# Stick-breaking's last gate tile computed among the first scores, and the second local attention's scores two steps at a time with its output projection spread

## The reference, cut to what matters

```python
# stick-breaking attention, per block of 128 queries
logits = jnp.einsum("bhtd,bhsd->bhts", q[:, :, s0:end], kb) * (Dh ** -0.5)
log_keep = jnp.where(mask, jax.nn.log_sigmoid(-logits), 0.0)
after = jnp.sum(log_keep, axis=-1, keepdims=True) - jnp.cumsum(log_keep, axis=-1)
wts = jnp.where(mask, jnp.exp(jax.nn.log_sigmoid(logits) + after), 0.0)
outs.append(jnp.einsum("bhts,bhsd->bhtd", wts, vb))
...
o = o * jax.nn.silu(z)                       # z: the gate, half of a projection of h
return o.astype(h.dtype) @ w_out

# second block
scores = jnp.einsum('nbqhd,nbkhd->nbhqk', qb, kb)      # + bias, softmax, lse
...
y_a = o * jax.nn.silu(g_a)
mixed = jnp.concatenate([y_f, y_a], axis=-1) @ w_out   # y_f: the Fourier half
h = h + mixed
```

## Time and profile before

| | us |
|---|---|
| median of 3 runs | 1233.19 |
| lowest and highest | 1231.24, 1233.85 |
| the profiled execution | 1230.61 |
| its span from first to last instruction | 1228.7 |
| TensorE busy in the span | 1176.3 (96%) |
| ScalarE busy | 538.8 (44%) |
| VectorE busy | 487.4 (40%) |
| GpSimd busy | 370.7 (30%) |

### The profile page before, as it was taken

One profiled execution on the slowest core, in us unless ns is written; L12 is line 12 of the kernel. 1 busy time (PEld: TensorE's weight loads), 2 busy tenths in 40 slices (PEclk: granted clock), 3 DMA queues, 4 the chain that ended last, 5 costly groups with the idle time before them and its releaser, 6 DMA issues.

```text
span 1228.7 us, 21193 instructions
## 1 busy us (share of the span) xinstructions
PE 1176.3 (96%) x8874; PEld 914.7 (74%) x8874; DVE 487.4 (40%) x919; ACT 538.8 (44%) x924; POOL 370.7 (30%) x148
## 2 busy tenths in 40 slices
PE   5999999999989999999999999999999999999998
PEld 3788886677668888777765666888887777777767
DVE  4575544544324472341314553640202332231462
ACT  4232237633336343543547774333125433754430
POOL 0143343132265314344331001332144122333250
PEclk8999999999999999999999999999999999999999
DMA  9723331356650232322422100323132321324201
GB/s 318 231 69 102 102 101 37 103 188 223 208 180 2 69 103 70 102 81 91 129 69 73 26 14 1 124 89 103 34 106 84 111 78 35 103 70 155 87 1 69
DMA packets 105761, 121.14 MB, mean 99 GB/s; under 512 B 5145, under 2 KB 91705, under 8 KB 105673
## 3 DMA queue, kind: packets, MB, share of 16 engines
q1 hardware_dynamic: 101424, 116.14, 29.9%
q10 hardware_dynamic: 4248, 3.73, 1.1%
HBM read 111.47 MB, written 2.10 MB: 92 GB/s over the span
## 4 chain that ended last, share of the span: by engine, by line
PE 84%; ACT 6%; DVE 4%; issue 3%; DMA 1%; ACTq 0%; SPq 0%; POOL 0%; DVEq 0%
PE ps L2039 42%; PE ps L2846 4%; PE ps L2644 3%; PE ps L2635 2%; PE ps L2180 2%; PE ps L2085 2%; PE ps L2426 2%; PE ps L2669 2%; PE ps L2648 1%; PE ps L2778 1%; PE ps L2123 1%; PE ps L2203 1%; PE ps L2256 1%; PE ps L2731 1%; PE ps L2453 1%
## 5 line engine op out<-in xcount | busy, mean ns | idle before, releaser
L604 POOL TENSOR_TENSOR wlo<-raw,whi 128x2048 fp32r<-128x2048 f32 x53 | 245.1, 4624 | 586.1 <-ACT whi L768 571.5
L768 ACT ACTIVATE whi<-raw 128x2048 fp32r<-128x2048 f32 x52 | 99.3, 1911 | 203.2 <-PE ps L2039 164.2
L610 POOL TENSOR_TENSOR wlo<-raw,whi 128x2048 fp32r<-128x2048 f32 x10 | 46.4, 4641 | 111.0 <-ACT whi L857 62.7
L1277 ACT ACTIVATE p<-sc,nmx 128x256 f32<-128x256 f32 x64 | 32.0, 501 | 49.6 <-PE ps L2765 29.5
L857 ACT ACTIVATE whi<-raw 128x2048 fp32r<-128x2048 f32 x11 | 21.1, 1918 | 62.7 <-PE ps L2039 62.7
L2039 PE MATMUL ps<-hC_hi,whi 128*128 128x512 f32 x184 | 47.1, 398 | 0.8 <-POOL wlo L604 0.8
L1861 DVE CUSTOM_DVE_ANT_0 sc<-ps,biast 128x256 f32<-128x256 f32 (+1 forms) x64 | 23.1, 394 | 62.2 <-PE ps L2756 33.3
L2039 PE MATMUL ps<-hC_lo,whi 128*128 128x512 f32 x184 | 45.5, 390 | 0.0
L2039 PE MATMUL ps<-hC_hi,wlo 128*128 128x512 f32 x184 | 45.4, 389 | 0.0
L2039 PEld LDWEIGHTS ps<-hC_hi,whi 128*128 128x128 f32 x184 | 33.8, 188 | 14.9 <-issue 6.4
L2039 PEld LDWEIGHTS ps<-hC_lo,whi 128*128 128x128 f32 x184 | 34.5, 188 | 7.4
(11 more groups left out here) (514 smaller groups left out, 2822.5 us busy)
## 6 DMA issues: line engine op xcount, KB each, us to landing
raw<-in_w_in_dram SPq DMA_DIRECT2D x24, 1024.0 KB, 5.2
raw<-in_w_in_a_dram SPq DMA_DIRECT2D x16, 1024.0 KB, 5.8
raw<-in_w_ada_dram SPq DMA_DIRECT2D x8, 1024.0 KB, 5.5
late_w<-in_w_ada_dram SPq DMA_DIRECT2D x8, 1024.0 KB, 5.5
raw<-in_w_kv_dram SPq DMA_DIRECT2D x8, 1024.0 KB, 5.1
raw<-in_w_in_b_dram SPq DMA_DIRECT2D x8, 1024.0 KB, 5.3
ada_a<-in_w_ada_dram SPq DMA_DIRECT2D x4, 1024.0 KB, 10.0
ada_b<-in_w_ada_dram SPq DMA_DIRECT2D x4, 1024.0 KB, 13.2
```

The costliest lines, as they stand in the source:

```text
L604: pool.tensor_tensor(wlo[:, s, :], raw[:, s, :], whi[:, s, :].bitcast(F32), ALU.subtract).then_inc(lo_ready, 1)
L610: pool.tensor_tensor(wlo[:, s, :], raw[:, s, :], whi[:, s, :].bitcast(F32), ALU.subtract).then_inc(lo_ready, 1)
L768: A(whi[:, s, :], raw[:, s, :], ACT.Copy).then_inc(hi_ready, 1)
L1277: A(p2[:, n % 2, 256 * e:256 * e + 256], sc2[:, n % 2, 256 * e:256 * e + 256], ACT.Exp, scale=-1.0, bias=nmx[:, grp, t, 2 * hp + e:2 * hp ...
```

## The change

1. The last gate tile goes to PSUM bank 7 in three parts of 8 matmuls: ahead of `qk(0)`, between `qk(0)` and `qk(1)`, and behind `qk(1)`. `qk(1)` no longer waits for its copy; DVE copies it after head 0's totals, and `weighted` of pair 1 waits for that copy.
2. ACT's split of the second unit of `D_OUTB` moves from behind head 1's absolute value to behind the exponentials of head 1, in the third turn of the loop.
3. DVE takes the absolute values of heads 0 and 1 ahead of head 0's other work, and the totals lose their two copies: PE now adds two pieces of 128 columns from `att` itself.
4. `weighted` is split as blocks 0 and 3, then 1 and 2.
5. The second window attention takes its scores two steps at a time. The residual of tiles 0 to 2 starts those tiles in its first three pairs, the Fourier half goes in pieces of 6 matmuls, and two thirds of the first `early_rows` fill its last turn. Its shares are begun behind the last copy, and the split of `D_OUT2 + 1` moves one step on.

Two steps' scores stand together, the 12 products are cut in two, and the residual is gone from the middle. The diff, cut to its core:

```diff
 # ScalarE
                 A(later_att(n), later_logits(n), ACT.Abs).then_inc(head_logged, 1)
-                if n == 1:
-                    next_hi(D_ZB + 1, 1)
...
                 if n:
                     head_weights(n - 1)
+                if n == 2:
+                    next_hi(D_ZB + 1, 1)
...
-            window_exps(1, qB, {7: (D_OUT2, 1), 12: (D_OUT2 + 1, 0)}, fourier_hi, stat_exps)
+            window_exps(1, qB, {7: (D_OUT2, 1), 13: (D_OUT2 + 1, 0)}, fourier_hi, stat_exps)
 # VectorE
-                copy(after1[:, 0:128], k2[:, 0:128])
-                TT(after1[:, 128:256], k2[:, 128:256], k3, ALU.add).then_inc(after_step, 1)
-                copy(after0[:, 0:128], k1[:, 0:128])
+                TT(after1[:, 0:128], k2[:, 128:256], k3, ALU.add).then_inc(after_step, 1)
+                TT(after0[:, 0:128], k1[:, 128:256], k2[:, 0:128], ALU.add)
                 dve.wait_ge(after_step, n + 1)
-                TT(after0[:, 128:384], k1[:, 128:384], after1[:, :], ALU.add).then_inc(after_done, 1)
+                TT(after0[:, 128:256], k1[:, 256:384], after1[:, 0:128], ALU.add).then_inc(after_done, 1)
+                if n == 0:
+                    dve.wait_ge(dense_full, 4 * (D_ZB + 2))
+                    dve.wait_ge(gate_done, 7)
+                    copy(zsT[:, KD - 1, :], ps[:, 7, :]).then_inc(gate_done, 1)
...
-                if not grp:
-                    transposed(14)
+                transposed(14)
+                transposed(15)
                 if last:
                     last()
-                transposed(15)
 # TensorE, stick-breaking
-            dense_block(D_ZB + 1, hB)
+            dense_unit(D_ZB + 1, 0, hB)
...
+            products_ch(D_ZB + 1, 1, 0, hB).then_inc(dense_full, 1)
...
+            last_gate(range(8))
...
-                if n < 2:
-                    pe.wait_ge(gate_done, 7 + n)
+                if n == 0:
+                    pe.wait_ge(gate_done, 7)
...
-                later(0, after0[:, :]).then_inc(sfx_first, 1)
-                later(1, after1[:, :])
+                later(0, 128, att(n, off[1], off[1] + 128), 128)
+                later(0, 256, after0[:, :], 256).then_inc(sfx_first, 1)
+                later(1, 128, att(n, off[2], off[2] + 128), 128)
+                later(1, 256, after1[:, :], 128)
...
             qk(0)
+            last_gate(range(8, 16))
             qk(1)
+            last_gate(range(16, 24))
...
-                    weighted((n - 3) // 2, range(1) if n % 2 else range(1, NT))
+                    weighted((n - 3) // 2, (0, 3) if n % 2 else (1, 2))
 # TensorE, the window attention
-                for n in range(18):
-                    if n < 16:
-                        scores(n)
-                        beside(n, 0)
-                    if 1 <= n <= 16:
-                        transposes(n - 1)
-                    if n < 16:
-                        beside(n, 1)
...
+                for m in range(9):
+                    if m < 8:
+                        pair_scores(m)
+                    beside(m, 0)
+                    if m:
+                        transposes(2 * m - 2)
+                    beside(m, 1)
+                    if m:
+                        transposes(2 * m - 1)
+                    beside(m, 2)
...
+                    if m:
+                        weighted_sums(2 * m - 2)
+                        weighted_sums(2 * m - 1)
...
+            def out_rows(m, place):
+
+                if (m, place) in ((0, 0), (1, 1), (2, 1)):
+                    bank_free(D_OUT2, m)
+                    residual(0, m, True)
+                elif 3 <= m <= 6 and place:
...
+                    fourier_rows(m - 3, place - 1)
+                elif (m, place) == (7, 1):
+                    residual(0, 3)
+                elif m == 8 and place:
...
+                    early_rows(0, range(4 * place - 4, 4 * place))
```

More of the change, by code:

```diff
@@ L1777, in yb_low, with magnitudes @@
                 TT(yB_lo[:, kt, :], ybt[:, kt % 2, :], yB_hi[:, kt, :].bitcast(F32), ALU.subtract).then_inc(yblo_done, 1)
-            dve.wait_ge(dense_full, 4 * (D_ZB + 2))
-            dve.wait_ge(gate_done, 7)
-            copy(zsT[:, KD - 1, :], dense[3]).then_inc(gate_done, 1)
-            for n in range(HB):
+            def magnitudes(n):
                 dve.wait_ge(qk_full, n + 1)
@@ L1787, in _ @@
                                   ALU.bitwise_and).then_inc(abs_first, 1)
+            magnitudes(0)
+            for n in range(HB):
+                if n == 0:
+                    magnitudes(1)
+                elif n >= 2:
+                    magnitudes(n)
                 if n >= 5 and n % 2:
@@ L2613, in _, with last_gate @@
             dense_unit(D_ZB, 1, hB, later_sums(SQ_QB + 4, G_QB + 4))
-            dense_block(D_ZB + 1, hB)
+            dense_unit(D_ZB + 1, 0, hB)
+            pe.wait_ge(lo_ready, 2 * (D_ZB + 1) + 2)
+            bank_free(D_ZB + 1, 2)
+            products_ch(D_ZB + 1, 1, 0, hB).then_inc(dense_full, 1)
+            def last_gate(qs):
+                hi, lo = unit(whi, 1, "ch"), unit(wlo, 1, "ch")
+                for q in qs:
+                    which, k = divmod(q, KD)
+                    w, x = ((hi, hB_hi), (lo, hB_hi), (hi, hB_lo))[which]
+                    last = mm(ps[:, 7, :], w[:, k, 128:256], x[:, k, :], start=q == 0, stop=q == 23)
+                    if q == 23:
+                        last.then_inc(dense_full, 1)
+            last_gate(range(8))
             pe.wait_ge(kqn_done, 16)
@@ L2698, in _ @@
                 if n == HB + 1:
[L2699 removed]
+                    weighted(KD - 1, (0, 3, 1, 2))
                 elif n >= 3:
[L2701 removed]
+                    weighted((n - 3) // 2, (0, 3) if n % 2 else (1, 2))
                 if n + 1 < HB:
@@ L2848, in half_tile, with whole_tile @@
                     last.then_inc(dense_full, 1)
-            window(0, half_tile)
+            def whole_tile(m, place):
+                if place < 2:
+                    half_tile(2 * m, place)
+                else:
+                    half_tile(2 * m + 1, 0)
+                    half_tile(2 * m + 1, 1)
+            window(0, whole_tile)
             pe.wait_ge(exp_done, 32)
@@ L2879, in _, with residual, fourier_rows @@
             mix = (mix_hi, mix_lo)
-            def residual(b, t):
+            def residual(b, t, start=False):
                 for c in range(4):
                     last = mm(out_bank(b, t)[:, 128 * c:128 * c + 128], xT[:, 4 * b + c, 128 * t:128 * t + 128], ident,
-                              start=False, stop=True, skip_group_check=True)
+                              start=start and c == 0, stop=True, skip_group_check=True)
                 return last
-            def fourier_rows(n, part):
-                if n in (6, 8, 10, 12) and part == 0:
-                    if n == 6:
-                        pe.wait_ge(lo_ready, 2 * D_OUT2 + 1)
-                        pe.wait_ge(mixlo_done, 4)
-                    t = (n - 6) // 2
-                    bank_free(D_OUT2, t)
-                    last = products_t(0, t, mix)
-                    if t == NT - 1:
-                        last.then_inc(half_done, 1)
-                elif n in (7, 9, 11, 13) and part == 0:
-                    residual(0, (n - 7) // 2)
-            window(1, fourier_rows)
+            def fourier_rows(t, half):
+                hi, lo = unit(whi, 0, "t"), unit(wlo, 0, "t")
+                for q in range(6 * half, 6 * half + 6):
+                    which, k = divmod(q, 4)
+                    x, w = ((mix_hi, hi), (mix_hi, lo), (mix_lo, hi))[which]
+                    last = mm(dense[t], x[:, k, 128 * t:128 * t + 128], w[:, k, :], start=t == 3 and q == 0, stop=False,
+                              skip_group_check=True)
+                if half and t == NT - 1:
+                    last.then_inc(half_done, 1)
             def early_rows(t, qs):
@@ L2925, in mixed_rows @@
                     for n, (x, w) in enumerate(((mix_hi, hi), (mix_lo, hi), (mix_hi, lo))):
-                        last = mm(dense[t], x[:, 4 + k, cols], w[:, k, :], start=False, stop=k == 3 and n == 2)
+                        last = mm(dense[t], x[:, 4 + k, cols], w[:, k, :], start=False, stop=k == 3 and n == 2,
+                                  skip_group_check=True)
                     if k == 3:
                         last.then_inc(dense_full, 1)
-            pe.wait_ge(lo_ready, 2 * (D_OUT2 + 1) + 1)
-            pe.wait_ge(sco_done, 64)
-            early_rows(0, range(4))
             pe.wait_ge(mixw_dve, 9)
```

111 lines of the change are left out of this document (47 added, 64 removed).

## The result

The changed kernel takes 1235.65 us (median of 10 executions, 1233.55 to 1238.90), the kernel before 1231.62 us (median of 10, 1229.99 to 1233.85). The ratio is 1.003 with a 95% interval of 1.0019 to 1.0040, so the change costs 2.3 to 4.9 us. The forecast was 1236.7 us, 3.5 us above the kernel before. It was right in sign and size, and its main step, the chain from the late split to head 4's scores, is the one that the experiments confirm best. Several of the smaller steps were not right.

The account below looks back on a forecast made before the run. TensorE, busy 1176.3 of 1228.7 us, was taken as the bound. Terms +3.8 + 1.7 - 1.2 - 0.3 - 0.5 = +3.5 us on 1233.2 gave 1236.7 us, range 1232.5 to 1240.

Parts of the forecast that it names:

- The gain at the start: Start of stick-breaking: gate tile in pieces and later weight split let ScalarE start head 2's scores 3.9 us earlier.
- The loss that follows: Head 4's scores: the later split delays pair 2's exchange by 9.0 us, TensorE waits 8 us; net +3.8 us.
- Rival A: Head 4's scores: pair 2's copies land in time, before 658.2, so no stall; -5.9 us, 1227.3 us; chance 12%.
- Rival B: Pair 2's exchange: DMAs late but landing sooner than 5.5 us after issue; 3.3 us less, 1233.4 us; chance 8%.
- The clock: Behind the stall at head 4's scores: TensorE falls to half clock, +1.7 us (bounds 0 and 1.8).
- rival C: Stall doesn't lower the clock, or the second window attention keeps full clock with free shares; 1235.0 us; chance 10%.
- The weighted sums: Head loop: blocks 1 and 2 end 0.2 us earlier than blocks 1 to 3, over 6 turns; -1.2 us.
- The last heads: End of the head loop: last heads have no cover on the weighted sums' path; -0.3 us (bounds -0.5 and 0).
- The window attention: Second window attention in pairs: 7.5 us of waits against 8.5 us lost before; -0.5 us taken, allowing for blocked shares.
- Rival D: Second window attention: thin opening or last turn lowers the clock again, 1.7 us, shares blocked, 0.9; 1239.3 us; chance 10%.
- The cut sums: Stick-breaking sums: two more matmuls per head for the same columns; a piece costs by its columns, so 0.
- rival E: Stick-breaking sums: the cut sums cost TensorE up to 6 us; 1242 us; chance 2%.

Follow-up runs that it names:

- the run alone: Kernel before with only the second window attention changed (two steps at a time): 1230.28 us, ratio 0.9993 to the kernel before.
- before_split_late: Kernel before with only ScalarE's weight split moved behind head 1's weights: 1241.42 us, ratio 1.0085 to the kernel before.
- the best version: Changed kernel with pair 2's exchange ahead of the load in SyncE's list, shares ahead of the last copy, sums as before: 1223.26 us, ratio 0.9923 to the kernel before.
- swap_first: Changed kernel with pair 2's four exchange DMAs ahead of the load in SyncE's list: 1225.50 us, ratio 0.9944 to the kernel before.

## Why the prediction was right, and where it was not

- **The gain at the start** (3.9 us) measured 4.10 us. The gate tile in pieces gives 3.62 of it by head 0's scores. That the split's going frees ScalarE was wrong for the kernel before, where it was hidden behind a wait for VectorE; what its going is worth in the new order is not shown.
- **The loss that follows** (+3.8 us) measured +3.91, with the wait (8 us, 7.7 measured), its cause and its place. Three runs show the chain from three sides: shorten it at SyncE, shorten it at ScalarE, or bring it into the old kernel. Rival A fell by its own condition, the landing; its size, 5.9 us faster than before, is what the change gives once SyncE's list has the way around (6.0 measured).
- **Rival B** (a landing sooner than 5.5 us after issue) fell: the last DMA, issued at 663.82, ended the wait at 669.44.
- **The clock** (+1.7 us) measured +1.8 between the two profiles (1.34 to head 4, 0.5 on the turn behind it) and 2.1 with the stall filled. The first half of rival C, no fall behind the stall, fell with it. Its second half was partly real: the second window attention kept the full clock in all ten profiles, and its shares were free in three of seven.
- **The weighted sums** (-1.2 us) measured -1.1 by the turns (five turns behind head 5 give 5.55 - 4.64 = 0.91, the one ahead of it 0.2). **The last heads** (-0.3 us) gave nothing: from head 15's absolute value to the projection's second part pass 14.1 us in both. The wait there is ScalarE's last exponential, 0.57 us against 0.55.
- **The window attention** (-0.5 us) was mis-sized as a mechanism, though the run alone fits its number. The 7.5 us of waits that I summed for the new order were too many: the changed kernel has 7.5 (54.4 us, of which 46.9 busy), but with blocked shares, which my sum left out; where the shares were free, 6.0 to 6.4. TensorE's busy time fell as well, from 48.5 us (before_split_late, at full clock throughout) to 47.0, where I had taken it as unchanged. And the step that took the old order's 5.1 us of waits and 3.4 us of clock as fixed failed: the wait for the values hangs on their landing, the clock's falls come and go, and the stretch varies by 6.7 us over four profiles. At full clock and with free shares the new order is only some 0.4 us shorter (53.1 us against 53.5 in the one profile of the old order without a fall), so that the run alone fits -0.5 is luck. Rival D (clock falls again, shares blocked) was real in parts: the shares were blocked in four of seven, the clock fell behind the attention in six of ten.
- **The cut sums** (0) measured +2.9 us alone and +1.8 in the best version, the latter not clear of noise. By the medians that step failed; by the rows of the head loop it holds, to 0.3 us. It did not fail by the rival's mechanism. The rule of the Trainium skill, "TensorE: Matmul & The Clock Gate", sections "LDWEIGHTS (loading the stationary operand)" and "The mechanism", would make it 6 us as an estimate, and it has no support in any row here: the pieces start 0.22 us apart, and rival E's six us did not come. I can't say what does cost the time.

The forecast was right in its two large terms, and they make most of the sum: the landing and the clock were forecast at +5.5 together, and the rows show +5.7. That the total came out at +3.5 against a measured +4.0 is in part luck: the gain of the window attention is larger than forecast in most pairs of profiles, and the cut sums cost something by the medians that no row shows. The two would nearly cancel, but neither is measured well enough to say so for certain.

## What to carry to other kernels

When a change moves one step later on an engine, follow what hangs on it through the other engines' queues, down to transfers that only stand behind it in a DMA list: here 9 us of delay passed from ScalarE to POOL to SyncE and came out at TensorE, and two lines in SyncE's list turned a loss of 4 us into a gain of 6. Before costing an edit by a stretch of one profile, ask whether its waits hang on a transfer whose start varies; where they do, the stretch has no fixed length. An edit that gains nothing alone may have been hidden behind a wait that another edit removes: look at what ends the wait behind it. And a repair should be tried with each part of the change taken out again: by the medians, the part that looked free was not.

## What the hardware showed that I had not expected

- **Unused work pays.** 7 us of products nobody reads, in a 7.7 us wait, kept TensorE at 2.4 GHz and made the kernel 3.9 us faster (1235.65 to 1231.78), 2.1 us of it visible in the rows behind the stall. Twice as much of it, which overran the wait, made the kernel 9.0 us slower than the changed one.
- **The same code takes different times in one kernel's executions.** Up to the first exchange the program is the same in all fourteen profiles, and they reach it between 596.9 and 603.6 us. Twelve executions of swap_first took 1220.1 to 1231.4 us: the three with a mean granted clock of 0.983 to 0.986 took 1229.6 us or more, the six at 0.992 and above 1226.5 or less. In between the order is loose: 0.990 went with 1230.0 and 0.989 with 1224.5.
- **A collision by a coin's flip.** VectorE's two 128x32 products took 0.29 or 1.65 us; they were started 0.08 to 0.09 us ahead of POOL's multiplication in seven profiles, were held until it had ended in four of them and ran freely in three.
- **Landing depends on what is in front.** In the changed kernel the last exchange of pair 2, issued behind a 1 MB load, landed 5.6 us after issue; the quickest of its kind in the same execution took 2.2 us.
